# How far ahead of TensorE the weight splits may run: a bound of four units becomes six

## What is computed

```
z = x @ w_in + b_in            # split into z_a, z_b, z_g, q, z_m
u = z_a[:, :512] * sigmoid(z_a[:, 512:]);  c_a = depthwise_conv31(u)
y_a = silu(layer_norm(c_a)) @ w_a_out
c_b = depthwise_conv4(z_b);  y_b = (rg_lru(c_b) * gelu(z_g)) @ w_b_out
y_c = attention(q, mem_k, mem_v) @ w_c_out
x = layer_norm(ALPHA * x + (sum_br sigmoid(z_m[br]) * y_br) @ w_mix_out)
x = layer_norm(ALPHA * x + ffn(x))
```

## Time and profile before

| | |
|---|---|
| median of 3 executions | 1924.13 us (1924.04 to 1924.48) |
| profiled execution | 1922.55 us, span 1920.8 us |
| TensorE (PE) busy | 1805.2 us, 94% |
| VectorE (DVE) busy | 1454.0 us, 76% |
| ScalarE (ACT) busy | 1050.4 us, 55% |
| mean granted TensorE clock | 0.977 |
| DMA, mean over the span | 233 GB/s |

### The profile page before, as it was taken

The page is one execution under the profiler, slowest core; times in us unless marked ns, Lnnn a source line. Parts: engine busy times, 40 slices in busy tenths (PEclk is TensorE's granted clock), DMA queues, the critical chain, the costliest instruction groups (busy, mean ns, idle before and its releaser), DMA issues.

```text
span 1920.8 us, 30248 instructions
## 1 busy us (share of the span) xinstructions
PE 1805.2 (94%) x11495; PEld 1564.1 (81%) x11496; DVE 1454.0 (76%) x2067; ACT 1050.4 (55%) x1191; POOL 146.2 (8%) x159
## 2 busy tenths in 40 slices
PE   7998999899999999899979979999999999999993
PEld 7887899799987988799957767878787888888782
DVE  6999686665535999867585667888888888886766
ACT  4453754543424544475354556677777676775553
POOL 2210000000000111000021001020202020100000
PEclk9999999899999999999989999999999999999997
DMA  7564344354443554534437779999999999896763
GB/s 266 201 229 179 119 145 142 110 167 152 154 143 112 194 213 146 208 132 144 132 116 261 266 289 338 360 355 349 355 357 350 366 341 377 330 386 219 278 241 91
DMA packets 119393, 447.10 MB, mean 233 GB/s; under 512 B 11056, under 2 KB 11184, under 8 KB 118784
## 3 DMA queue, kind: packets, MB, share of 16 engines
q1 hardware_dynamic: 112288, 424.45, 60.3%
q0 software_dynamic: 7008, 21.34, 3.5%
HBM read 435.68 MB, written 12.67 MB: 233 GB/s over the span
## 4 chain that ended last, share of the span: by engine, by line
PE 39%; issue 4%; DVE 3%; ACT 2%; DMA 2%; POOLq 0%; DVEq 0%; SPq 0%; POOL 0%; ACTq 0%
PE psum L2053 12%; PE psum L2054 11%; PE psum L2055 11%; PE psum L2077 2%; ACT wph L639 2%; DMA e_ring<-experts 1%; DVE wpl L645 1%; PE psum L2109 1%; PE psum L2118 1%; PE psum L1767 1%; DVE hT L1711 0%; DVE stats L1201 0%; DMA out_acc<-arena,rows_out 0%; DMA x<-out_acc 0%; DVE arena L1704 0%
## 5 line engine op out<-in xcount | busy, mean ns | idle before, releaser
L645 DVE TENSOR_TENSOR wpl<-e_ring,wph 128x2048 fp32r<-128x2048 f32 x269 | 607.1, 2290 | 95.9 <-ACT wph L639 95.0
L639 ACT CAST wph<-e_ring 128x2048 fp32r<-128x2048 f32 x269 | 502.2, 1904 | 138.2 <-DMA e_ring<-experts 69.6
L589 DVE TENSOR_TENSOR wl<-ring,wh 128x1024 fp32r<-128x1024 f32 x234 | 285.1, 1223 | 198.9 <-ACT wh L583 198.2
L1781 PE MATMUL psum<-xTh,wh 128*128 128x320 f32 x1184 | 376.6, 318 | 35.9 <-DVE wl L589 19.8
L1782 PE MATMUL psum<-xTl,wh 128*128 128x320 f32 x1184 | 371.2, 314 | 0.0
L1783 PE MATMUL psum<-xTh,wl 128*128 128x320 f32 x1184 | 370.9, 313 | 0.0
L583 ACT CAST wh<-ring 128x1024 fp32r<-128x1024 f32 x234 | 243.6, 1046 | 157.8 <-PE psum L1802 71.8
L2053 PE MATMUL psum<-wph,xe 128*128 128x512 f32 (+1 forms) x768 | 297.0, 387 | 16.4 <-issue 13.4
L2054 PE MATMUL psum<-wph,xe 128*128 128x512 f32 (+1 forms) x768 | 292.1, 380 | 0.0
L2055 PE MATMUL psum<-wpl,xe 128*128 128x512 f32 (+1 forms) x768 | 290.1, 378 | 0.0
L1781 PEld LDWEIGHTS psum<-xTh,wh 128*128 128x128 f32 x1184 | 227.2, 192 | 48.3 <-DVE wl L589 28.6
(11 more groups left out here) (323 smaller groups left out, 2272.7 us busy)
## 6 DMA issues: line engine op xcount, KB each, us to landing
e_ring<-experts SPq DMA_DIRECT2D x264, 1024.0 KB, 6.1
ring<-stream SPq DMA_DIRECT2D x274, 512.0 KB, 3.3
lnp<-rows POOLq DMA_DIRECT2D x4, 1024.0 KB, 5.9
x<-x POOLq DMA_DIRECT2D x3, 512.0 KB, 5.5
arena<-x0T SPq DMA_DIRECT2D x2, 640.0 KB, 5.9
o_a<-arena POOLq DMA_DIRECT2D x2, 540.0 KB, 3.9
o_k<-arena POOLq DMA_DIRECT2D x2, 512.0 KB, 6.9
o_v<-arena POOLq DMA_DIRECT2D x2, 512.0 KB, 8.5
```

The costliest lines, as they stand in the source:

```text
L589: dve.tensor_tensor(wl[:, q % SPLITS, :], ring[:, u % SLOTS, :], wh[:, q % SPLITS, :].bitcast(F32), ALU.subtract).then_inc(lo_done, 1)
L639: act.copy(wph[:, SLOT_OF[m % NPOS], :], ring_place(m).rearrange("p u c -> p (u c)")).then_inc(hi_e, 1)
L645: dve.tensor_tensor(wpl[:, s, :], ring_place(m).rearrange("p u c -> p (u c)"), wph[:, s, :].bitcast(F32), ALU.subtract).then_inc(lo_e, 1)
L1781: pe.matmul(out, h[:, k], hi[:, k], start=(k == 0), stop=False)
```

## The change

The second bound of `near` becomes the units done plus `SLOTS`, which is 6, in place of `2 * AHEAD`, which is 4. The first bound stays. Nothing else is edited. The same function is used by ScalarE's and VectorE's programs.

```
         def near(u, step):
 
             return (plan.split[u] < sum(done <= step for done in split_steps) + AHEAD and
-                    u < sum(done <= step for done in plan.unit_done) + 2 * AHEAD)
+                    u < sum(done <= step for done in plan.unit_done) + SLOTS)
```

## The result

The changed kernel took 1928.09 us, the median of 20 executions, against 1924.09 of 20 of the kernel before: a ratio of 1.0022 (95% interval 1.0015 to 1.0029), by the ratio 4.2 us slower, interval 2.9 to 5.6; the two medians are 4.0 us apart. In a later set it was 1.0018 (1.0009 to 1.0027). The sign is as forecast and 1928.1 lies in the range; 5.8 us had been forecast. The profiled execution took 1929.60 us, span 1927.8, which is 7.0 more than that of before. Single executions of either kernel differ by more than the change does: the 20 of the changed kernel run from 1922.8 us (mean granted clock 0.978) to 1932.7 (0.974). So sizes are taken from medians, and the profiles tell where.

What follows compares the result with a forecast made beforehand. TensorE was taken as the bound, busy 1805.2 of 1920.8 us. Layer 0 (0 + 1.1 + 2.1 = 3.2) and layer 1 (0.5 + 2.1 = 2.6) gave +5.8 us, a median of 1930.0 us, range 1925.5 to 1934.0.

Steps and rivals of the forecast that it cites:

- The sign: Whole kernel: the change makes it slower, by 5.8 us or +0.3%.
- The places: ScalarE's and VectorE's programs: 16 of 234 splits, the same eight in each layer, go one to a few places earlier.
- zb 4 and zg 0: Early mixing part: both waits for wl go, VectorE idles 3.8 us in layer 0; gain 0 there, 0.9 us in layer 1.
- The carry of 0 for layer 0: Layer 0 up to zg 3: gains are given back as VectorE sets the pace; net 0, bounds -0.4 to +0.6 us.
- g0 and g1: Start of the attention part: waits of 3.24 and 3.49 us go; g3 waits about 1 us, at 170.4, 4.9 us ahead.
- g4: Attention part: g4 waits for ot 0's bank, freed by samples_lo(0) behind two moved subtractions: +1.1 us layer 0, +0.5 layer 1.
- rival B: Faster: ot 0's bank isn't what g4 waits for, so it starts with its wl at 176.6: 1914 us, chance 0.07.
- The clock: Behind the new 7 us gap ahead of g4, TensorE runs at 1.2 GHz: 2.1 us a layer, +4.2 together, bounds 0 to 5.2.
- The sum: Whole kernel: layer 0 3.2 us, layer 1 2.6 us, together +5.8 us, median 1930.0 us; chance 0.60.
- rival A: Clock holds, falls in one layer only, or a low stretch elsewhere goes: 1925.7 to 1927.8 us, chance 0.22.

Runs made afterwards that it cites:

- The exchange of banks: Changed kernel with the PSUM banks of g4 and the mean exchanged, no instruction moved: 0.9967 of the kernel before, 1917.9 us.
- the kernel with the freeing put first: Changed kernel with samples_lo(0) moved on VectorE from n = 3 to n = 2, ahead of g4's subtraction: 0.9946 of the kernel before, 1913.3 us.
- the freeing alone: Kernel before, its bound of four kept, with samples_lo(0) moved to n = 2: ratio 0.9994, 1923.4 us.
- load of zg 6 held: Changed kernel with SyncE waiting ahead of zg 6's load until zg 2 has landed: 1.0018 of the kernel before, 1928.0 us.

## Why the prediction was right, by its steps

**The places.** All eight waits behind raw units were for wl, and the bound moved the eight splits a layer that were named: the waits of zb 4, zg 0 and g0 are gone, in both layers.

**zb 4 and zg 0.** VectorE stood for zb 4's cast as said, for 2.45 us where 3.8 was forecast. The carry of 0 for layer 0 (bounds to +0.6) is the term that was mis-sized in the profile: zg 3 began at 132.10, some 0.6 us later than before (three blocks of 3.57 us behind zg 0's start at 120.83, 131.5), and behind its gap the clock fell, so ob 0 ended 2.2 us later (g0's start, 160.45, against 161.52 - 3.24 = 158.28). The reason was another than VectorE's wait at zb 4, which the working had weighed: with zb 4 and zb 5 alone zg 3 isn't late. The working had let the load for zg 2 land 3.5 us from issue, and its last part landed after 5.2. In the medians this costs nothing that can be told: 0.9988 for these splits alone. In layer 1, the 0.9 us are there: from zb 0 to g2's subtraction it is 777.76 - 697.44 = 80.32 us, against 772.63 - 691.43 = 81.20 before, where g2's is the last of these three:

```profile
770.16 3.70 DVE L589 TENSOR_TENSOR wl<-ring,wh 128x1024 fp32r<-128x1024 f32 x3
```

**g0 and g1** went without waits, and g3 after a short one (0.84), as said; g3 at 172.55 and not 170.4, by the 2.2 us lost ahead of g0.

**g4** was the step that decided. Its mechanism held, and so did its size, counted from g2's subtraction. From g2's subtraction to samples_lo(0) VectorE took 180.63 - 162.92 = 17.71 us before and 184.73 - 165.12 = 19.61 after: +1.9, where 2.3 less 0.3 was forecast. In layer 1 it is 797.38 - 777.76 = 19.62, +2.3 as forecast. Counted from the start of the kernel g4 is 3.1 us later in layer 0 (185.16 against 182.10) where 1.1 was forecast, as the chain itself began 2.2 us later and not 0.3. The exchange of banks shows that g4 waited for the bank; the kernel with the freeing put first shows that with it free the 10 us of rival B are to be had.

**The clock.** Forecast 2.1 us a layer. From g4 to yc 0: 2.66 us more in layer 0, and (820.15 - 797.81) - (811.88 - 791.45) = 1.91 in layer 1: 4.6 together, 4.2 forecast. Keeping TensorE busy gave back some 4 us by the ratios. Of what the Trainium skill says (TensorE: Matmul & The Clock Gate, "What's actually happening", that the ramp penalty is under 1% of a typical kernel's span and that a model shouldn't be fitted to a count of slow matmuls) the size agrees for these two gaps, 4.6 of 1928 us; but it was more than half of what the change cost in the profiled executions, and without it the forecast would have been "no change".

**The sum.** 5.8 us forecast, 4.2 measured by the ratio, 7.0 between the two profiled executions. In those the two mixing parts, from zb 0 to yc 0, are 5.95 us (208.26 - 202.54, plus 0.23 as zb 0 began that much earlier) and 2.26 us longer; what comes behind yc 0 of layer 1 takes 1.3 us less. The low clock doesn't explain these 1.3 us: TensorE is busy for 1043 us there in both, and only its idle time is shorter. That 5.8 lies near either number is in part luck, as the 2.2 us ahead of g0 in layer 0 were not in it. What stays open is which part of the clock's term the typical execution pays: the change without g4 and g5 says less than the profiles do. (The range's lower end, 1925.5, is called that of rival A, which by its own sum is 1925.7.)

## What to carry to other kernels

When a wait is taken away, ask of the waiting block everything else that it needs, its output buffer too, and who frees that. An instruction put earlier in an in-order queue puts all behind it later; what it passes may be the release that someone waits for. And a gap that grows on TensorE is to be priced twice, for its length and for the clock behind it.

## What the runs showed of the hardware

In the mixing parts of the fourteen traces the granted clock fell at every gap of TensorE from 3.44 us up to 6.98. At gaps from 1.87 to 3.31 us it did either. It fell at 1.87 us (the change without g4 and g5, zg 3), 1.93 (zb and zg alone, g0 of layer 0), 2.21 (the freeing alone, g4), 2.27 (the change, zg 3) and 3.10 (g4 and g5 alone, g4). It held at 2.16 (load of zg 6 held, zg 3), 2.27 (zg 0 and zg 1 alone, zg 3), 2.98 (zb 4 and zb 5 alone, g0 of layer 1) and 3.31 (zb and zg alone, g0 of layer 1), and at the 1.34 and 1.83 of before. With the banks exchanged, two gaps of nearly one length parted: 2.66 in layer 0 held, 2.67 in layer 1 fell. The row of the longest gap at which it held, and the stretches of that gap and behind it:

```profile
775.43 0.41 PE L1783 MATMUL psum<-xTh,wh 128*128 128x320 f32 x1 [3.31 <-DVE wl L589]
...
774.00:775.40 1.40, 0.00 (x0) 0.00 (x0) 1.40 (x4) 0.00 (x0) 0.00 (x0) 1.00 0.99 389
775.40:777.00 1.60, 1.57 (x10) 1.57 (x11) 1.29 (x2) 1.27 (x3) 0.00 (x0) 1.00 1.02 402
```

So the length of a gap alone doesn't tell here whether the clock falls. Filling the two gaps with matmuls whose result nobody uses was worth some 4 us.

The load for zg 2, 512 KB, took 3.3 to 3.8 us from issue to its last landing in the five traces without a packet of instructions beside it, and 4.7 to 5.3 in the nine with one, where one part of 16 came late.

Twelve executions of one program spread over 6 to 8 us. In the 20 of the changed kernel the time goes with the mean granted clock (correlation -0.88), so low stretches that come or stay away are a likely reason; in its later 11 it hardly does (-0.10). A profile is one draw of them.
